# Delta core: half-column level steps with the two heads of a pair of iterations side by side

## The reference

```
L = where(strict, (k*beta) @ k.T * decay, 0)
sol = triangular_solve(eye + L, [v*beta, k*beta*exp(g)])      # u, w
qk = where(tril, q @ k.T * decay, 0)
# scan over chunks:
v_new = u - w @ S ;  o = (q*exp(g)) @ S + qk @ v_new
S = S * exp(g_last) + (k*exp(g_last - g)).T @ v_new
```

## Time and profile before

| what | value |
|---|---|
| median of 3 runs (lowest, highest) | 5612.43 us (5612.35, 5614.2) |
| span of the profiled execution | 5611.9 us |
| busy over the whole span: PE, DVE, ACT, POOL | 84%, 59%, 38%, 39% |
| first DMA of the delta core | 1840.2 us |
| last copy of an output in it | 3931.7 us |
| VectorE busy in slices 17 to 28 of 40, in tenths | 8 |
| DMA queue of loads and stores, share of 16 engines | 29.7% |

### The profile page before, as it was taken

The page is one execution under the profiler, slowest core; times in us unless marked ns, Lnnn a source line. Parts: engine busy times, 40 slices in busy tenths (PEclk is TensorE's granted clock), DMA queues, the critical chain, the costliest instruction groups (busy, mean ns, idle before and its releaser), DMA issues. The chain is left out here.

```text
span 5611.9 us, 92238 instructions
## 1 busy us (share of the span) xinstructions
PE 4687.5 (84%) x32058; PEld 3852.9 (69%) x32058; DVE 3332.0 (59%) x3990; ACT 2146.1 (38%) x3371; POOL 2161.1 (39%) x1544
## 2 busy tenths in 40 slices
PE   7479889988998688888888888888599759975649
PEld 1467777777777577777777777777488548864547
DVE  1414543455334688888888888888455443339854
ACT  0212222232223455555555555555211231137732
POOL 0311111111121666777666767675211132213222
PEclk8569999999999899999999999999799879987879
DMA  4102212212222333333333333332544212221134
GB/s 203 48 25 70 58 49 69 81 46 64 65 69 62 92 95 95 92 92 92 95 95 94 92 93 93 95 93 77 186 174 177 102 54 68 66 94 69 67 103 135
DMA packets 587420, 503.28 MB, mean 90 GB/s; under 512 B 115200, under 2 KB 556544, under 8 KB 573184
## 3 DMA queue, kind: packets, MB, share of 16 engines
q1 hardware_dynamic: 587296, 501.82, 29.7%
HBM read 351.00 MB, written 150.67 MB: 89 GB/s over the span
## 5 line engine op out<-in xcount | busy, mean ns | idle before, releaser
L448 PE MATMUL pj_bank<-h_hi,pj_whi 128*128 128x512 f32 (+1 forms) x1920 | 716.5, 373 | 19.7 <-POOL pj_wlo L434 19.7
L448 PE MATMUL pj_bank<-h_lo,pj_whi 128*128 128x512 f32 (+1 forms) x1920 | 707.8, 369 | 0.0
L448 PE MATMUL pj_bank<-h_hi,pj_wlo 128*128 128x512 f32 (+1 forms) x1920 | 707.3, 368 | 0.0
L1215 DVE TENSOR_TENSOR dc_Y<-dc_psY,dc_levels 128x512 f16<-128x512 f32 x864 | 554.3, 683 | 117.3 <-PE dc_psY L996 113.8
L1219 DVE TENSOR_TENSOR dc_X<-dc_psX,dc_X 128x512 f16<-128x512 f32 x864 | 575.8, 690 | 79.6 <-PE dc_psX L1010 48.4
L431 POOL TENSOR_TENSOR pj_whi<-pj_w,ones 128x1024 fp32r<-128x1024 f32 x48 | 126.8, 2642 | 1192.4 <-DMA pj_w<-in_gdn_w_in 959.0
L1129 ACT ACTIVATE dc_R<-dc_psR 128x512 f16<-128x512 f32 x864 | 492.5, 596 | 123.2 <-PE dc_psR L1006 112.8
L622 ACT ACTIVATE pj_raw<-pj_bank 128x512 f32<-128x512 f32 (+1 forms) x240 | 129.0, 555 | 1005.6 <-PE pj_bank L448 634.9
L448 PEld LDWEIGHTS pj_bank<-h_hi,pj_whi 128*128 128x128 f32 x1920 | 362.9, 189 | 82.9 <-POOL pj_wlo L434 20.1
L912 POOL TENSOR_TENSOR dc_bm<-dc_dec,dc_bm 128x512 f32<-128x512 f32 x144 | 183.3, 1273 | 588.1 <-ACT dc_dec L1106 587.9
L448 PEld LDWEIGHTS pj_bank<-h_lo,pj_whi 128*128 128x128 f32 x1920 | 363.0, 189 | 62.6 <-issue 3.8
(11 more groups left out here) (239 smaller groups left out, 11155.3 us busy)
## 6 DMA issues: line engine op xcount, KB each, us to landing
dc_tm<-scratch_tm SPq DMA_DIRECT2D x288, 192.0 KB, 2.4
dc_fm<-scratch_fm SPq DMA_DIRECT2D x288, 128.0 KB, 2.6
dc_cgr<-scratch_cgrow SPq DMA_DIRECT2D x288, 128.0 KB, 2.9
scratch_o<-dc_ob SPq DMA_DIRECT2D x288, 128.0 KB, 1.9
scratch_tm<-pj_tm SPq DMA_DIRECT2D x24, 1152.0 KB, 6.3
mod_w<-in_mod_w SPq DMA_DIRECT2D x16, 1536.0 KB, 30.2
pj_w<-in_gdn_w_in SPq DMA_DIRECT2D x48, 512.0 KB, 7.4
scratch_fm<-pj_row SPq DMA_DIRECT2D x16, 1152.0 KB, 6.0
```

Source lines behind the costliest of these rows:

```text
L448: i = pe.matmul(self.bank[blk][:, 0:n], l[b][:, k, :], r[:, k, at:at + n], start=(m == 0), stop=(m == 3 * KT - 1))
L1215: dve.tensor_tensor(Y[p][:], bY[p][:], lev_r(l + 1), ALU.mult).then_inc(eY[p], 1)
```

## The change

Two heads are now side by side: p = 0 and p = 1 are the same chunk of two different query/key heads, each with its own state, right side and faded state. 4 pairs of heads times 18 chunks are again 72 iterations with the same work in each. There is one bank bV for Gram product, solve and outputs, and one bank bZ for k S and the update, in turns of p = 0 and p = 1.

A level now computes only the half of the columns that it changes. The identity is added to L once (A = Lhi + 1), and each level has its own Y tile that already holds the identity, so that the new R and the new X come out of one product each and the identity matmul is gone. Levels 2 to 6 move 64 columns per matmul (128x256 per p), level 1 moves 64 for Y and 128 for R and X. Copies write strided columns (`all_cols`). VectorE masks Y of both heads, copies X of both at level 1, and X of p = 1 at levels 2 to 6; ScalarE copies R of both and X of p = 0. The q part of the Gram product is masked on VectorE (`masked`, 128x512) where ScalarE copied it; GpSimd has `beta_decay` in place of L907, L912 and L913. The scores now read two SBUF tiles. SyncE's loop is unrolled, with the same 28 DMAs in an iteration, in a new order. VectorE builds masks and Y tiles once at the start (26 small operations).

```diff
--- before.py
+++ after.py
@@ def phase_delta_core(nc, sem, T, io, dram): @@
+    NI = NSTEP // 2
...
+        A, Llo = four("A", C4, F16), four("Llo", C4, F16)
+        X0, X, R, YN = (two(x, C4, F16) for x in ("X0", "X", "R", "YN"))
+        R0 = two("R0", H4, F16)
+        Y = [two(f"Y{l}_", C4, F16) for l in range(1, NLEV)]
...
+        bY, bR, bX = ([bank(f"{x}{p}") for p in range(2)] for x in "YRX")
+        bZ, bV = bank("Z"), bank("V")
...
+        def cols(t, c, l, own):
+            o = (c // 2 == 0) == own
+            return comb(t, c).rearrange("p (b o s) -> p b o s", o=2, s=1 << l)[:, :, 1 if o else 0, :]
+        def all_cols(t, l, of_r):
+            s = 1 << l
+            at, step = (s, 2 * P - s) if of_r else (0, 2 * P + s)
+            a = t[:]
+            return bass.AP(tensor=a.tensor, offset=a.offset + at, ap=[[4 * P, P], [step, 2], [2 * s, P // s], [1, s]])
...
+                def step(m, n, last):
+                    for load, ahead in ((load_rec, 1), (load_fm, 3), (load_row, 4)):
+                        if not (last and n + ahead >= NCH):
+                            for p in range(2):
+                                load(*place(m, n, ahead), p)
+                    for p in range(2):
+                        store(m, n, p)
...
+                    pool.tensor_tensor(bd[p][:], dec[q][p][:], tok(gi[q][p], Q_BETA), ALU.mult).then_inc(s_bd[p], 1)
...
                 @sweep
                 def run(i, q, ahead, make, inv, rec):
+                        beta_decay(i + 2, q, 0)
+                    if inv:
+                        attention(i + 1, 1 - q, 0)
+                    if make:
+                        beta_decay(i + 2, q, 1)
+                    if inv:
+                        faded_q(i + 1, 1 - q, 0)
                     if rec:
                         faded_state(i, q, 0)
                     if inv:
                         attention(i + 1, 1 - q, 1)
                     if rec:
                         faded_state(i, q, 1)
                     if inv:
+                        faded_q(i + 1, 1 - q, 1)
+                    for p in range(2):
+                        if ahead:
+                            differences(i + 3, 1 - q, p)
+                        if make:
+                            low(i + 2, q, p)
+                        if inv:
+                            beta_v(i + 1, 1 - q, p)
...
+                def level_y(j, q, l, p):
+                    if l == 1:
+                        pe.wait_ge(eF[p], j + 1)
+                    else:
+                        pe.wait_ge(eR[p], j * U + l - 1)
+                    for c in range(4):
+                        m = pe.matmul(quart(bY[p])[:, c * 64:(c + 1) * 64], comb(A[q][p], c),
+                                      half(R0[p], c) if l == 1 else cols(R[p], c, l, True), start=True, stop=True)
+                    m.then_inc(pY[p], 1)
+                def level_rx(j, l, p):
+                    y = Y[l - 1][p]
+                    pe.wait_ge(eY[p], j * LV + l)
+                    if l == 1:
+                        wait(pe, eR[p], j * U)
+                        wait(pe, eX[p], j * U)
+                    else:
+                        pe.wait_ge(eX[p], j * U + l - 1)
+                    for c in range(4):
+                        if l == 1:
+                            m = pe.matmul(comb(bR[p], c), comb(X0[p], c), comb(y, c), start=True, stop=True)
+                        else:
+                            m = pe.matmul(quart(bR[p])[:, c * 64:(c + 1) * 64], comb(X[p], c), cols(y, c, l, True), start=True, stop=True)
+                    m.then_inc(pR[p], 1)
+                    for c in range(4):
+                        if l == 1:
+                            m = pe.matmul(comb(bX[p], c), comb(y, c), comb(X0[p], c), start=True, stop=True)
+                        else:
+                            m = pe.matmul(quart(bX[p])[:, c * 64:(c + 1) * 64], comb(y, c), cols(X[p], c, l, False), start=True, stop=True)
                     m.then_inc(pX[p], 1)
...
+                def solved(i, p):
+                    pe.wait_ge(s_xr[p], i + 1)
+                    pe.wait_ge(eR[p], (i + 1) * U)
+                    if p == 0:
+                        wait(pe, s_gm[1], i + 3, NI)
+                    else:
+                        pe.wait_ge(s_vn[0], i + 1)
+                        pe.wait_ge(s_vs[0], i + 1)
...
+                    for l in range(1, NLEV):
                         if inv:
                             for p in range(2):
                                 level_y(j, r, l, p)
+                        if rec and l <= 2:
+                            state_by_k(i, q, l - 1)
+                        if rec and l in (3, 4):
+                            solved(i, l - 3)
+                        if rec and l == 6:
+                            update(i, q, 1)
                         if inv:
                             for p in range(2):
                                 level_rx(j, l, p)
+                        if make and l <= 2:
+                            gram(i + 2, q, l - 1)
+                        if rec and l == 4:
+                            update(i, q, 0)
+                        if rec and l >= 5:
+                            outputs(i, q, 0, l - 5)
...
+                def level_r(j, l, p):
+                    act.wait_ge(pR[p], j * U + l)
+                    if l == 1:
+                        act.activation(R[p][:], bR[p][:], ACT.Copy).then_inc(eR[p], 1)
+                    else:
+                        act.activation(all_cols(R[p], l, True), split4(quart(bR[p]), l), ACT.Copy).then_inc(eR[p], 1)
+                def level_x(j, l, p):
+                    act.wait_ge(pX[p], j * U + l)
+                    act.activation(all_cols(X[p], l, False), split4(quart(bX[p]), l), ACT.Copy).then_inc(eX[p], 1)
...
+                        decays(i + 2, q, 0)
+                    for l in range(1, NLEV):
+                        if inv:
+                            for p in range(2):
+                                level_r(j, l, p)
+                            if l > 1:
+                                level_x(j, l, 0)
+                        if rec and l in (3, 4):
+                            new_v(i, l - 3)
+                        if make:
+                            if l == 1:
+                                decays(i + 2, q, 1)
+                            elif l <= 3:
+                                growth(i + 2, q, l - 2)
+                            elif l <= 5:
+                                high(i + 2, l - 4)
...
+                def masked(j, q, p):
+                    dve.wait_ge(p_gram[p], j + 1)
+                    wait(dve, s_qk[p], j - 1)
+                    dve.tensor_tensor(gm[q][p][:], bV[:], sides[:], ALU.mult).then_inc(s_gm[p], 1)
+                def scores(j, q, p):
+                    dve.wait_ge(s_bd[p], j + 1)
+                    wait(dve, s_llo[p], j)
+                    dve.wait_ge(s_gm[p], j + 1)
+                    dve.tensor_tensor(L32[p][:], heads(gm[q][p][:, :, 0, :]), bd[p][:], ALU.mult).then_inc(s_L[p], 1)
+                def first(j, q, p):
+                    dve.wait_ge(s_lhi[p], j + 1)
+                    wait(dve, pX[p], (j - 1) * U)
+                    dve.tensor_tensor(flat(A[q][p]), flat(Lhi[p]), id16[:], ALU.add).then_inc(s_A[p], 1)
+                    dve.wait_ge(s_A[p], j + 1)
+                    wait(dve, pX[p], (j - 1) * U + 1)
+                    dve.tensor_tensor(X0[p][:], A[q][p][:], heads(x0m[:]), ALU.mult).then_inc(s_x0[p], 1)
+                def level(j, l, p):
+                    dve.wait_ge(pY[p], j * U + 1 + l)
+                    dve.tensor_tensor(all_cols(Y[l - 1][p], l, True), split4(quart(bY[p]), l),
+                                      split4(pick[:, l - 1].rearrange("p c t -> p (c t)"), l), ALU.mult).then_inc(eY[p], 1)
+                def level_x(j, p):
+                    dve.wait_ge(pX[p], j * U + 1)
+                    dve.tensor_copy(X[p][:], bX[p][:]).then_inc(eX[p], 1)
+                def half_x(j, l, p):
+                    dve.wait_ge(pX[p], j * U + l)
+                    dve.tensor_copy(all_cols(X[p], l, False), split4(quart(bX[p]), l)).then_inc(eX[p], 1)
...
+                            if l == 1:
+                                for p in range(2):
+                                    level_x(j, p)
+                        if rec and l == 1:
+                            right_side(i, q, 0)
+                        if rec and l in (3, 4):
+                            faded_v(i, q, l - 3)
+                        if make and l in (1, 2):
+                            masked(i + 2, q, l - 1)
+                        if rec and l == 2:
+                            right_side(i, q, 1)
+                        if make and l in (3, 4):
+                            scores(i + 2, q, l - 3)
+                        if make and l in (5, 6):
+                            first(i + 2, q, l - 5)
```

(10 more changed lines are left out.)

556 lines of the change are left out of this document (226 added, 330 removed).

## The result

The changed kernel takes 5351.95 us (median of 4 runs, 5347.76 to 5357.34) against 5613.32 for the kernel before beside it: ratio 0.9534, 95% interval 0.952 to 0.9547.

What follows compares the result with a forecast made beforehand. VectorE bound the old iteration, TensorE close behind; afterwards order decides. A 23.5 us walk plus lock waits gave 25.3 for 28.55, 231 us off 5611.9, 5385 with a few for the start; range 5250 to 5510, likeliest 5310 to 5440.

Steps and rivals of the forecast that it cites:

- Period: Delta core's iteration, timed by the last copy of the inverse: 25.3 us forecast for 28.55 before.
- the lock: VectorE and GpSimd operations reading two SBUF tiles exclude each other: 3.9 us of waits an iteration, about 1.9 on the path.
- The walk without contention: One delta-core iteration followed in order, with forecast durations and 0.05 per hand-off: 23.5 us.
- the term for the 64-column matmuls: TensorE in the levels: each 64-column matmul taken at 0.045 us, between 0.028 and 0.055.
- Shapes: Prices of 256-column operations: VectorE mask 0.42 us, VectorE copy 0.40, ScalarE half copy 384 ns.
- Start and tail: Outside the steady part: 5 to 8 us of added start work against a shorter first sweep and tail, about 0.
- 1, no cost of the lock: VectorE's idle times absorb the VectorE-GpSimd waits: 23.5 to 24.3 us an iteration, 5250 to 5310 us; 18%.
- 2, walk too tight: Delta core has more waits than the hand count sees: 26.3 to 28.2 us, 5450 to 5590; 23% with lower clock.
- 3, strided columns: Half operations of VectorE and ScalarE no cheaper for hopping over column blocks: 30.5 us an iteration, 5750 us; 5%.
- 4, the clock: TensorE's clock partly at 1.2 GHz; at 0.92, 26.1 us an iteration, 5440 us; shares 23% with too few waits seen.
- 5, 64 columns at 0.055: TensorE's 64-column matmuls cost as much as 128-column ones: 1.4 us more work, inside the range; no chance of its own.
- what would show it: Signs listed for the profile after: period, group means, operations stretched by GpSimd, TensorE's waits, and a clock of 1.00.

Runs made afterwards that it cites:

- e11_park2: Changed kernel with two GpSimd waits: last faded q after VectorE's scores of p = 0, differences, Llo and beta v after X0 of p = 1; 5210.32 us.
- e8_ident_back: Changed kernel with a 512-column identity matmul put back ahead of each R product, its result overwritten; 5440.25 us.
- e1_park: Changed kernel with GpSimd holding differences, Llo and beta v back until VectorE has written X0 of p = 1; 5219.5 us.
- e3_state_first: Changed kernel with VectorE's new state of p = 0 moved ahead of A and X0 in level 5; 5351.79 us.
- e5_park_act: Changed kernel with GpSimd's differences, Llo and beta v held until X0 of p = 1, and all half X copies on ScalarE; 5190.37 us.

## Why the prediction was right

**Period.** 25.3 said, 24.98 measured (24.87 in the iterations at full clock); 231 us said, 253.5 measured. The mechanism was right: the half columns shorten the iteration, and the lock, at the places named, takes some of that back. Three of its sizes were off, and in part they offset each other, so that the closeness of the sum is partly luck.

**The walk without contention** had 23.5; e11_park2, where scores, A and X0 are not stretched, has 22.65 at full clock, 0.85 less. The first suspect is the term for the 64-column matmuls. I took 0.045 between bounds of 0.028 and 0.055; the rows show 0.030. Ten levels of one head with twelve such matmuls each, 0.015 less on each, is 1.8 us less TensorE work. e8_ident_back has about half of added TensorE work reach the period, which would be 0.9. That is an estimate, and no run changes this term alone.

**The lock** was sized at 3.9 us of waits with 1.9 on the path (its sum used 1.8). It was 3.4 with 2.0, or 2.2 at full clock. Two errors in it offset each other. A and X0 were given 3.5 us of waits and had 2.5, but 2.1 of these count (e1_park), where the prediction let about half count. The scores were given 0.4 and had 0.9, of which under 0.2 counts (e11_park2). The stated places were right: faded q in front of scores 0, Llo in front of A, beta v in front of X0. The Trainium skill, "SBUF — State Buffer", section "SBUF: two separate sides", has the loser wait for the whole instruction of the other; the trace agrees where the two start together (1.41 for an A of 0.42 beside a Llo of 1.16), and e1_park shows that keeping them apart gives the time back.

**Shapes.** Masks 413 (0.42 said), half copies 410 (0.40), ScalarE's 383 (384).

**Start and tail** "about 0": the first sweep ended 8.1 us earlier. The clock in its stretch was 0.77 of full speed, where the kernel before had 0.92, and it was ahead in spite of it. Of the 33 us between forecast and result, 23 are the period, 8 this, and the rest lies within the few us that were added for the start.

**The rivals.** 1, no cost of the lock: that VectorE's idle time absorbs it fell with e1_park, apart from the scores; a kernel without the lock is at 22.99, below even this rival's range. 2, walk too tight: it fell; the levels start within 0.4 us of the walk, and without the lock the walk is too long. 3, strided columns: it fell at 413 ns; the Trainium skill's "Advanced Engine Details and Errata", section "Memory Cachelines", wants two hits in a 16-byte line, which even the shortest runs here give, and the trace agrees, at level 1's masks as at level 6's (404 to 425 ns for all 864). 4, the clock: it came true in a small way. At 0.98 in the steady part it costs some 11 us here (0.1 an iteration) and some 21 in e11_park2, and comes in whole stretches at half speed, not as a constant loss. 5, 64 columns at 0.055: it fell at 0.030.

**Wrong** in "what would show it": a clock of 1.00 (0.98). Most values of scores, A and X0 above 1000: the medians are 717, 783 and 1148, since the scores of p = 1 run free and A of p = 1 meets only the end of a Llo. Llo above 1.16: it stayed at 1.16, and of the two only beta v rose (1.22). And I named level 6's products and the second Newton product as TensorE's waits. The longest is that of the update for the new state; e3_state_first shows that it and the two I named are one wait in different places. The 2.05 us that VectorE idles at the seam were in the walk (outputs, Newton and last product, 18.7 to 23.5) but not named as a bound.

## What to carry to other kernels

When an operation count falls and the engines stay below full, look at the mean of each small group against the price of its shape: a mean of two to three times the least duration can be a wait that the page counts as work (here A, 984 for 416 ns). Where VectorE and GpSimd both read two tiles of SBUF, look at which of them run at the same moment, and let the one with slack wait on purpose; here two waits on GpSimd, idle for a third of the time, gave another 142 us on top of the change's 261. A wait's length says little of its price: 2.5 us of waits in levels 5 and 6 cost 1.8 to 2.1, 0.9 in level 3 cost under 0.2, and a 1.6 us wait of TensorE, once removed, came back in two other places. After each edit, compare the means of the stretched groups and the iterations at the same clock before the time is credited to the edit: the 29 us of e5_park_act over e1_park are 0.08 us an iteration at full clock.

## What the runs showed of the hardware

A 64-column f16 matmul with a new 128x128 weight load takes 0.030 us in groups of four, where one of 128 columns takes 0.055: the load does not set a floor above 0.030. Copies out of PSUM to f16 columns in runs of 2, 4, up to 64 cost no more than plain ones (404 to 425 ns for 256 columns). A VectorE operation that meets GpSimd ends its own duration less 0.14 us behind GpSimd's end (0.28 for A and X0, 0.55 for the scores, 1.08 for L1910); in proportion that is most for the f16 operations of 0.42 us, up to 1.41. Whether they meet depends on phase: moving 0.9 us of TensorE's products and one copy of ScalarE brought the scores from 712 to 1107 ns with nothing changed in VectorE's or GpSimd's order. TensorE's clock of 0.98 was 1.00 with stretches of a few us at 0.50, and an iteration of the same instructions took 24.28 us with such a stretch and 22.63 without (e11_park2).
